# Turning activation blocks by transposing DMAs instead of TensorE transposes, in a one-layer hybrid decoder step on 8 cores

## The reference, cut to what matters

```
h = x + 0.5 * rmsnorm(swiglu(rmsnorm(x, g1), w_gate, w_up, w_down), g1post)    # FFN 1, width 2816
n = rmsnorm(h, gm)
b_a | c_a | h_a | u | v = n @ w_in                                              # 5 x 512 columns
y_a = b_a * causal_dwconv3(c_a * h_a)
v_n = rmsnorm(v per head of 64);  y_b = u * (tril(W_s[head]) @ v_n + b_s)       # chunks of 128 positions
h = h + rmsnorm(concat(rmsnorm(y_a), rmsnorm(y_b)) @ w_out, gmpost)
h = h + 0.5 * rmsnorm(swiglu(rmsnorm(h, g2), ...FFN 2 weights...), g2post)
y = h + rmsnorm(sigmoid(h @ ple_w_gate) * (p @ ple_w_proj), gple)
```

## Time and profile before

| | us |
|---|---|
| median of 3 runs | 1431.52 (1430.39 to 1508.89) |
| the profiled execution, own time | 1431.39 |
| its span, slowest of 8 cores | 1430.4 (cores 1427.1 to 1430.4) |
| TensorE busy | 1325.6 (93%) |
| VectorE, ScalarE, GpSimd busy | 523.9, 465.9, 95.2 |
| granted TensorE clock, mean by core | 0.972 to 0.977 |

### The profile page before, as it was taken

The page is one execution under the profiler, slowest core; times in us unless marked ns, Lnnn a source line. Parts: engine busy times, 40 slices in busy tenths (PEclk is TensorE's granted clock), DMA queues, the critical chain, the costliest instruction groups (busy, mean ns, idle before and its releaser), DMA issues.

```text
span 1430.4 us, 19034 instructions; the slowest of 8 cores (1427.1 to 1430.4 us)
## 1 busy us (share of the span) xinstructions
PE 1325.6 (93%) x7028; PEld 664.3 (46%) x7028; DVE 523.9 (37%) x690; ACT 465.9 (33%) x906; POOL 95.2 (7%) x187
## 2 busy tenths in 40 slices
PE   4899999999989999999992999999998999999994
PEld 1466654445545666644440444444443444444442
DVE  1322223337676222222364321223366831222236
ACT  2311113444456211122382211123343731111245
POOL 2110000010000000000100000000100000000000
PEclk9999999999999999999995999999999999999997
DMA  9996321069046443320499455330694255532002
GB/s 223 206 212 100 66 45 30 1 116 159 13 85 106 70 79 59 60 45 1 58 233 236 141 97 89 50 55 1 110 163 67 43 100 94 89 53 52 0 16 118
DMA packets 34331, 126.53 MB, mean 88 GB/s; under 512 B 4416, under 2 KB 4672, under 8 KB 33600
## 3 DMA queue, kind: packets, MB, share of 16 engines
q0 software_dynamic: 25296, 90.25, 39.0%
q1 hardware_dynamic: 8944, 35.05, 7.6%
HBM read 206.03 MB, written 9.51 MB: 151 GB/s over the span
## 4 chain that ended last, share of the span: by engine, by line
PE 83%; ACT 5%; DMA 5%; DVE 4%; issue 3%; POOL 0%; ACTq 0%; DVEq 0%; SPq 0%; POOLq 0%
PE ps L217 54%; PE ps L536 23%; PE ps L525 3%; ACT big L222 2%; DMA y<-big 2%; DMA ring<-w 2%; PE ps L310 1%; DVE big L230 1%; DVE big L226 1%; DMA big<-xT 1%; DVE nT L226 1%; ACT nT L222 1%; DVE zsc L226 1%; ACT L222 1%; ACT st L222 0%
## 5 line engine op out<-in xcount | busy, mean ns | idle before, releaser
L217 PE MATMUL ps<-nT,ring 128*128 128x384 bf16 (+1 forms) x4160 | 790.6, 352 | 22.6 <-DVE nT L226 8.9
L217 PEld LDWEIGHTS ps<-nT,ring 128*128 128x128 bf16 x4160 | 410.2, 99 | 399.0 <-issue 53.5
L230 DVE TENSOR_TENSOR big<-ps,sg 128x384 bf16<-128x384 f32 (+1 forms) x220 | 134.2, 611 | 516.5 <-PE ps L217 491.2
L536 PE MATMUL ps<-ring,big 128*128 128x512 bf16 x1320 | 289.1, 379 | 4.5 <-DVE big L230 4.5
L222 ACT ACTIVATE sg<-ps 128x384 f32<-128x384 f32 (+1 forms) x237 | 127.0, 537 | 505.1 <-PE ps L217 503.4
L536 PEld LDWEIGHTS ps<-ring,big 128*128 128x128 bf16 x1320 | 128.0, 98 | 155.7 <-issue 6.1
L255 POOL DMA_DIRECT2D ring<-w x170 | 90.3, 536 | 1255.6 <-PE ps L217 669.3
L222 ACT ACTIVATE big<-ps 128x1024 bf16<-128x1024 f32 (+4 forms) x91 | 78.8, 874 | 230.2 <-PE ps L536 195.0
L226 DVE SCALAR_TENSOR_TENSOR zsc<-ps,st,gains 128x1024 f32<-128x1024 f32 x51 | 65.4, 1283 | 206.0 <-ACT st L222 205.7
L536 PE MATMUL ps<-ring,nT 128*128 128x512 bf16 x480 | 106.5, 379 | 2.2 <-DVE big L230 2.2
L230 DVE TENSOR_TENSOR big<-ps,big 128x384 f32<-128x384 f32 (+3 forms) x80 | 54.3, 707 | 66.1 <-PE ps L217 44.0
(11 more groups left out here) (65 smaller groups left out, 432.3 us busy)
## 6 DMA issues: line engine op xcount, KB each, us to landing
ring<-w POOLq DMA_DIRECT2D x170, 512.0 KB, 9.8
h<-x SPq DMA_DIRECT2D x17, 512.0 KB, 24.4
y<-big SPq DMA_DIRECT2D x16, 512.0 KB, 7.0
gains<-gain SPq DMA_DIRECT2D x12, 512.0 KB, 13.5
h<-xT SPq DMA_DIRECT2D x3, 1536.0 KB, 17.6
big<-xT SPq DMA_DIRECT2D x2, 2048.0 KB, 14.6
big<-pT POOLq DMA_DIRECT2D x2, 512.0 KB, 11.8
big<-wsT SPq DMA_DIRECT2D x1, 512.0 KB, 23.5
```

Source lines behind the costliest of these rows:

```text
L217: ins = nc.tensor.matmul(out_ap, l, r, start=(i == 0), stop=(i == n - 1))
L230: return DVE.mark(nc.vector.tensor_tensor(out=out, in0=in0, in1=in1, op=op))
L536: ins = nc.tensor.matmul(o.t, lhs(k), sv, start=(k == 0), stop=(k == nk - 1))
```

## The change

The block is written to a ring of two buffers of its own (`nbr_t`) instead of into the hidden buffer. Right after `pre` or `cast`, `emit_T` has SP issue one transposing DMA from that buffer to `nT_t`; SP first waits for the block and for the transposing DMA before it. `pre` and `cast` wait until the DMA of two blocks before has read the buffer that they write. `nT_ev[b]` is the DMA's completion. No block is turned on TensorE, no bank is used and nothing is evicted for it; the lags and the places of the later turns fall away. `ev_T`, for which the mixer's convolution and the next pass's first input load wait, is the last transposing DMA. To make room, the output buffer of the conv state shares the memory of the loaded one (`ncv_t = sct_t`).

```diff
-    ncv_t = nc.alloc_sbuf_tensor("ncv", [128, 4, 32], F32)
+    ncv_t = sct_t
...
+    nbr_t = nc.alloc_sbuf_tensor("nbr", [128, 2, 8, 128], BF16)
+    nbr_ev = [None, None]
+    nbr_n = {"i": 0}
+
+    def nbr():
+        i = nbr_n["i"] % 2
+        nbr_n["i"] += 1
+        return i, nbr_t[:, i, :, :]
...
-    def queue_T(b, src, wait):
-        tq.append((b, src, wait))
+    def queue_T(b, src, wait, ri):
+        tq.append((b, src, wait, ri))
+
+    t_sem = [DmaSem(nc, "t%d" % b) for b in range(9)]
+    t_last = {"ev": None}
 
     def emit_T(bank_of, on_act=True):
-        b, src, wait = tq.pop(0)
-        bank = bank_of()
-        o = bank.t.bitcast(BF16).rearrange("p (k s) -> p k s", k=8)
-        PE.wait(wait, ev_ident)
-        ins = None
-        for k in range(8):
-            ins = nc.tensor.transpose(o[:, k, :], src[:, k, :], ident_t[:])
-        ev = PE.mark(ins)
-        dst = nT_t[:, :, b * 128:(b + 1) * 128]
-        if on_act:
-            e = act([ev], out=dst, in_=o, func=AF.Copy)
-        else:
-            e = copy_v([ev], dst, o)
-        bank.free = e
-        nT_ev[b] = e
-        return ev
+        b, src, wait, ri = tq.pop(0)
+        SP.wait(wait, t_last["ev"])
+        e = t_sem[b].add(nc.sync.dma_start(out=nT_t[:, :, b * 128:(b + 1) * 128], in_=src, transpose=True))
+        nT_ev[b] = nbr_ev[ri] = t_last["ev"] = e
+        return e
...
-            while tq and any(b not in nT_ev for b in P.blocks(ti)):
-                emit_T(get_bank)
...
-            if ti == 0:
-                while tq:
-                    ev_T = emit_T(get_bank)
+            ev_T = t_last["ev"]
...
-                e_ncv = copy_v([zev], ncv_t[:].rearrange("p c (q s) -> p c q s", q=16), zs[:, :, :, 8:10])
+                e_ncv = copy_v([zev, ev_zs], ncv_t[:].rearrange("p c (q s) -> p c q s", q=16), zs[:, :, :, 8:10])
...
-        ev_T = None
+        ev_T = t_last["ev"]
...
         def pre_mid(gi, j0):
             def f(b, ev_d):
-                e = pre(b, gi, nb(b, j0), ev_d)
-                queue_T(b, nb(b, j0), e)
+                ri, dst = nbr()
+                e = pre(b, gi, dst, [ev_d, nbr_ev[ri]])
+                queue_T(b, dst, e, ri)
+                emit_T(None)
...
         def cast(b, ev_d):
-            e = copy_v([h_ev[b], ev_d], nb(b, 14), h_t[:, b, :].rearrange("p (k s) -> p k s", k=8))
-            queue_T(b, nb(b, 14), e)
+            ri, dst = nbr()
+            e = copy_v([h_ev[b], ev_d, nbr_ev[ri]], dst, h_t[:, b, :].rearrange("p (k s) -> p k s", k=8))
+            queue_T(b, dst, e, ri)
+            emit_T(None)
```

More of the change, by code:

```diff
@@ L832, in ple @@
                 while tq and b not in nT_ev:
-                    ev_T = emit_T(get_tp)
+                    pass
                 pair, ev = proj_block(P, b, 8, lambda k, b=b: nT_t[:, k, b * 128:(b + 1) * 128], 4, fg, [nT_ev[b]],
```

## The result

The changed kernel takes 1458.22 us (median of 4 runs, 1454.93 to 1459.4) against 1430.92 for the kernel before (3 runs): ratio 1.0187, 95% interval 1.0166 to 1.0208. It is slower by 27 us where 20 us less were forecast.

The account below looks back on a forecast made before the run. TensorE, busy 93% of the span and 83% of the chain, was taken as the bound; -17.9 - 4.3 - 4.8 + 0.9 + 3.5 + 2.0 = -20.6 from 1431.39 us gave 1411 us, range 1402 to 1472.

Parts of the forecast that it names:

- What goes: Transposes in TensorE's stream (-17.9 us) and the waits at the mixer starts of pass 0 (-4.3) and pass 1 (-4.8): -27.0.
- T: Landing time of one transposing DMA, taken as 4.3 us, hidden in down projections and hardly in the quiet output projections.
- the +0.9: Output projection of pass 0: loss in us at T = 4.3 from the next stage's banks being freed late.
- The moved rotation in pass 1: Stage after pass 1's output projection: its first bank falls on block 7's pair, freed late by VectorE, +3.5 us.
- The formula with T = 3.1: Loss 4T - 13.7 for the first bank after pass 1's output projection; +3.5 us at T = 4.3.
- T in the loaded stretches: Landing beside weight loads: 9.5 us at the pass boundary; at mixer starts covered up to about T = 13, costing nothing.
- The output projection called quiet: Output projections have little DMA traffic (share 0.01 at 430 to 440), so the short T of 4.3 us was used.
- the formula 7T - 29.2: Loss in the output projection of pass 0: nothing up to T = 4.17, +0.9 us at 4.3.
- the +2.0: Pass boundary: pass 1's first input load goes out at 721.7, 3.6 us late; 2.0 us of that taken as loss.
- D: Rival, chance 0.08: T short in quiet, but last blocks' DMAs land in 24.4 us where weight loads restart; 1444 us.
- B: Rival, chance 0.20: the turn is slow, T = 9.5, and output projections run at the DMA's pace; 1472 us.
- E: Rival, chance 0.05: all landings hide and output projections go at VectorE's pace; 1402 us.

Follow-up runs that it names:

- e10: Changed kernel, weight loads set free by each projection's last block (first load spared only in second down projection) held until the last transposing DMA lands: 1400.62 us, ratio 0.9787.
- e8: Changed kernel without SP's wait for the transposing DMA before, so two can be in flight: 1458.57 us, ratio 1.0184.
- e4: Changed kernel with the same DMAs copying plainly instead of transposing, in the same 256 B pieces: 1454.95 us (one run).
- e3: Changed kernel with each weight load cut in two by columns, packets of 2 KB instead of 4 KB: 1467.41 us, ratio 1.0265.

## Why the prediction was wrong, point by point

- **What goes: right.** Both mixer starts run without their wait, and in a down projection of the changed kernel the 352 matmuls of eight blocks take 76.15 us, 9.52 a block against 9.95. With all loads held back the span falls by 30.7 us (1430.4 to 1399.7), against 27.0 in the sum. The slow landings then cost 57.3, which makes the 26.6 measured.
- **T in the quiet: right in kind, too long.** 4.3 was put, 3.1 measured, and ScalarE's wait for the DMA in the output projections was there, at 0.2 to 0.5 us. So the output projections go at VectorE's pace, 3.72 us a block where 3.87 was named. In pass 0 the +0.9 did not come: in e10 the stages up to the second down projection gain 4.3 us, of which three blocks' transposes explain 1.3 and the pace 7 x 0.41 = 2.9.
- **The moved rotation in pass 1: right, though the changed kernel's landings hide it.** The loss of 3.5 was forecast since the next stage's first bank would be that of block 7's pair. TensorE does wait there, 6.81 us for VectorE's `zsc` of that block, and the granted clock behind it is 0.89 where it was 1.00:

```profile
1172.25 8.04 PE L226 MATMUL ps<-nT,ring 128*128 128x512 bf16 x27 [6.81 <-DVE zsc L235]
...
1172.00:1192.00 20.00, 19.75 (x83) 8.52 (x84) 6.31 (x8) 7.28 (x14) 0.70 (x1) 0.89 0.84 131
...
1144.00:1164.00 20.00, 19.60 (x109) 9.70 (x110) 7.81 (x9) 10.75 (x19) 0.70 (x1) 1.00 0.82 137
```

  (An instruction, then a stretch of each kernel, the changed one and the one before.) The start is 35.3 us behind that of the output projection, against 1142.7 - 1108.92 = 33.8 before: +1.5, and 20 x 0.11 = 2.2 for the clock. The formula with T = 3.1 would give a gain of 1.3; with the real pace of 3.72 in T's place it gives 1129.0 + 14.9 - 1142.7 = +1.2. The stage is 2.2 us longer than before in e10 too.
- **T in the loaded stretches: the step that failed.** The prediction priced a loaded landing by the row of 256 KB, 9.5 us, used that in its sum at the pass boundary alone, and put the mixer starts at nothing, as covered. The cover of 13 us was right (307.0, when the last block is ready, to 320.0, when TensorE stops), but the last block's DMA landed 29.6 us after 307.0. Two things were wrong. The size: the first landing of a pair took 29 to 31 us. Rows of DMAs whose packets are 2 to 4 KB don't price one in packets of 256 B, since the engines alternate by packets: most of its time under load is its number of packets per engine times the other queue's turn, 23 of 31 us here. And the place: it is the last block but one that meets the loads, and the last lands behind it, with SP's wait or without (e8). So "up to about T = 13 that is covered" stood against 31.37 + 7.54 = 38.9 us from the first issue. Worth 20.7 and 23.8 us by the table of e10.
- **The output projection called quiet.** The share of 0.01 held at 430 to 440; the loads that the last block sets free came under the DMA of the sixth block of nine. TensorE is ahead of the prenorms there, which makes "the last block's release" earlier than "the last blocks' turn". Worth 13.4 us, of which the formula 7T - 29.2 had nothing, as it took one T for all blocks.
- **The pass boundary: the +2.0 did not come.** The first input load went out at 758.49, not 721.7, 40 us after the kernel before. Yet from the second down projection to the next pass's first the changed kernel takes 314.49 us and e10, whose landings are all short, 314.67. The saturated stretch swallowed the delay (counted from the second down projection, the load goes out at +118.3 us there and at +94.3 in e10), all of it and not a part, within the few us by which cores differ there.
- **The rivals.** D had the mechanism, landings stretched where the weight loads restart, and 0.08 of the chance. It put 11 and 6 us at the mixer starts, 18 at the boundary and nothing in an output projection, where 20.7, 23.8, nothing and 13.4 came. Its objection, that the transposes don't queue behind one another, was the wrong one: they do, by the change's own rule, and queueing was not what made the first of them slow. B was what the range's upper end of 1472 came from; its T of 9.5 in the quiet did not occur, so that 1458 lies inside the range is luck. E priced VectorE's pace at 2 us a pass and put it into its sum once. Nor does the estimate from the Trainium skill, "VectorE: DVE Perf Modes", section "The three transpose paths", hold here: at 1309 ns for each 128x128 square eight would take 10.5 us, and eight land in 3.1. What the prediction set beside it, that a turning DMA is about as fast as a plain one, does hold: 3.1 against 2.9 us (e4).

The evidence for the alternation is the equal counts in three kernels, the landing that shrinks with the other queue's packets (e3), and its indifference to the turn (e4).

## What to carry to other kernels

In this kernel a DMA's landing under load went by how many packets it has, not by its bytes. Before you put a strided or turning DMA on a path, count its packets per engine, multiply by the turn measured beside whatever bulk load can run with it, add a few us (23 and 8 here), and look at what the schedule sets free at that very moment. Latency that matters and bulk that doesn't can be kept apart by one wait on the bulk's queue. The median landing of a new DMA says little; read its maximum, and its place in the chain. A long landing need not cost anything, as at the pass boundary here, so compare stage by stage with a version in which it is short.

## What the runs showed of the hardware

A DMA that turns a 128x1024 bf16 block from SBUF to SBUF landed in 3.0 to 3.1 us with quiet engines, the plain copy in the same 256 B pieces in 2.9; issuing it held SP for 1217 ns, where a plain one took 593. Behind the loads of three weight tiles both took 27 to 31 us, with packets one for one, and the second of two in flight (e8) kept SP for 15.9 us. Packets of 2 KB instead of 4 KB on the other queue shortened a turn from 0.363 to 0.205 us. In the two stretches of 40 and 35 us where TensorE waited for these landings the granted clock was 0.79 and 0.72.
